# The second one-hot table of the gate spread: one comparison on VectorE, its four parts multiplied by the gates on ScalarE

## The reference

```python
fv, fpos = lax.top_k(cand.reshape(T, PEER_HEADS, PEER_TOPK * PEER_TOPK), PEER_TOPK)
gates = jax.nn.softmax(fv, axis=-1).astype(h.dtype)
u = jnp.take(U, ic, axis=0)
act = jax.nn.gelu(jnp.einsum('chkd,cd->chk', u, xc), approximate=False)
vv = jnp.take(V, ic, axis=0)
return jnp.einsum('chk,chkd->cd', gc * act, vv)
```

## Time and profile before

| | |
|---|---|
| median of 3 runs | 2122.65 us (2121.01 to 2124.01) |
| the profiled execution: time, span | 2123.55 us, 2121.8 us |
| mean granted TensorE clock | 0.961 |
| busy over the span | PE 90%, PEld 75%, DVE 67%, ACT 35%, POOL 27% |

### The profile page before, as it was taken

One profiled execution on the slowest core, in us unless ns is written; L12 is line 12 of the kernel. 1 busy time (PEld: TensorE's weight loads), 2 busy tenths in 40 slices (PEclk: granted clock), 3 DMA queues, 4 the chain that ended last, 5 costly groups with the idle time before them and its releaser, 6 DMA issues.

```text
span 2121.8 us, 33140 instructions
## 1 busy us (share of the span) xinstructions
PE 1911.8 (90%) x10322; PEld 1599.3 (75%) x10322; DVE 1424.2 (67%) x2902; ACT 733.0 (35%) x1304; POOL 569.5 (27%) x435
## 2 busy tenths in 40 slices
PE   2889896786877999999999999996999999999995
PEld 2343585675733787879999999996998888888884
DVE  4187535435334577775688888884768888888886
ACT  1221224333312343435444444341243333333331
POOL 3011422031101232314422322323424333333311
PEclk9999998998988999999999999998999999999998
DMA  7373100000050333334699988889979999999981
GB/s 265 103 247 100 40 1 1 0 0 0 0 210 30 116 112 110 120 100 155 226 305 301 304 300 300 288 277 342 342 273 413 354 357 357 349 350 361 354 284 53
DMA packets 244203, 434.82 MB, mean 205 GB/s; under 512 B 84578, under 2 KB 157636, under 8 KB 244164
## 3 DMA queue, kind: packets, MB, share of 16 engines
q1 hardware_dynamic: 207300, 300.12, 40.9%
q0 software_dynamic: 36864, 134.23, 17.6%
HBM read 379.77 MB, written 54.53 MB: 205 GB/s over the span
## 4 chain that ended last, share of the span: by engine, by line
PE 64%; DMA 1%; DVE 1%; issue 1%; ACT 0%; POOL 0%; SPq 0%; POOLq 0%; ACTq 0%; DVEq 0%
PE bank L1318 25%; PE bank L1709 8%; PE bank L1710 8%; PE bank L1711 8%; PE bank L1298 5%; PE bank L1646 5%; PE bank L1692 4%; DMA urows<-in_peer_u 1%; PE bank L1658 1%; DMA gates<-SS 0%; POOL wide L1626 0%; DVE n_stats L1118 0%; DVE wide L2012 0%; DVE wide L2010 0%; DVE wide L1128 0%
## 5 line engine op out<-in xcount | busy, mean ns | idle before, releaser
L1318 PE MATMUL bank<-hh,uh 128*128 128x384 f32 x1024 | 358.3, 350 | 0.0
L1318 PE MATMUL bank<-hl,uh 128*128 128x384 f32 x1024 | 344.6, 337 | 0.0
L1709 PE MATMUL bank<-vh,wh 128*128 128x512 f32 x768 | 299.1, 389 | 3.1 <-DVE wl L1971 3.1
L1711 PE MATMUL bank<-vh,wl 128*128 128x512 f32 x768 | 299.0, 389 | 0.0
L1710 PE MATMUL bank<-vl,wh 128*128 128x512 f32 x768 | 299.0, 389 | 0.0
L1376 POOL DMA_INDIRECT vsel<-in_peer_v,picks x128 | 153.6, 1200 | 425.5 <-DVE gt L1402 411.5
L1805 ACT ACTIVATE vh<-vraw 128x1024 fp32r<-128x1024 f32 x128 | 135.9, 1061 | 287.7 <-PE bank L1711 272.6
L1376 POOL DMA_INDIRECT usel<-in_peer_u,picks x108 | 146.7, 1359 | 247.5 <-DVE usel L1383 233.9
L1968 DVE TENSOR_TENSOR vl<-vraw,vh 128x1024 fp32r<-128x1024 f32 x128 | 156.7, 1224 | 81.7 <-ACT vh L1805 81.7
L1318 PE MATMUL bank<-hh,ul 128*128 128x384 f32 x1024 | 198.4, 335 | 0.0
L1318 PEld LDWEIGHTS bank<-hl,uh 128*128 128x128 f32 x1024 | 194.4, 190 | 0.0
(11 more groups left out here) (314 smaller groups left out, 3106.2 us busy)
## 6 DMA issues: line engine op xcount, KB each, us to landing
urows<-in_peer_u SPq DMA_DIRECT2D x128, 512.0 KB, 7.8
vraw<-in_peer_v SPq DMA_DIRECT2D x128, 512.0 KB, 6.1
ada<-in_ada_w SPq DMA_DIRECT2D x12, 2048.0 KB, 8.7
scored<-act_out SPq DMA_DIRECT2D x128, 192.0 KB, 4.2
gates<-SS SPq DMA_DIRECT2D x16, 1536.0 KB, 13.0
gtile<-gates SPq DMA_DIRECT2D x32, 768.0 KB, 7.3
act_in<-scored SPq DMA_DIRECT2D x128, 192.0 KB, 6.2
wt<-in_w_in SPq DMA_DIRECT2D x19, 512.0 KB, 3.9
```

Source lines behind the costliest of these rows:

```text
L1318: last = pe.matmul(bank, u[:, k, :], h[:, k, :], start=(n == 0), stop=(n == 3 * KD - 1))
L1709: pe.matmul(b, wh[s][:, cols], vh[s][:, half], start=first, stop=False)
L1711: last = pe.matmul(b, wl[s][:, cols], vh[s][:, half], start=False, stop=stop)
```

## The change

VectorE makes all four parts of OJ with one comparison of 128x512, as it did for OI, and raises a new semaphore `ones_up`. ScalarE, once it has copied row s+1, waits for it, multiplies the four parts of each step of row s in place by their gates, and raises `hot`, on which TensorE waits as before.

```diff
@@ ScalarE, for each row s, behind the copies of row s+1 and the small Gelu
+                        for q in steps_of(s):
+                            n = STEPS * (i - SPREAD) + q
+                            act.wait_ge(ones_up, START + n + 1)
+                            for k in range(4):
+                                last = act.activation(OJ[q % SLOTS][:, k, :], OJ[q % SLOTS][:, k, :], ACT.Copy,
+                                                      scale=turned[2][:, bass.ds(4 * n + k, 1)])
+                            last.then_inc(hot, 1)
                         for q in steps_of(s):
                             act.wait_ge(spread, START + 2 * STEPS * b + (STEPS * o + q + 1))
@@ VectorE, hot_step
-                for k in range(4):
-                    at = bass.ds(4 * n + k, 1)
-                    last = dve.tensor_scalar(OJ[q % SLOTS][:, k, :], iota[:, :], turned[1][:, at], turned[2][:, at],
-                                             ALU.is_equal, ALU.mult)
-                last.then_inc(hot, 1)
+                dve.tensor_tensor(OJ[q % SLOTS], iota[:, :].unsqueeze(1).broadcast_to([P, 4, P]),
+                                  turned[1][:, bass.ds(4 * n, 4)].unsqueeze(2)
+                                  .broadcast_to([P, 4, P]), ALU.is_equal).then_inc(ones_up, 1)
```

More of the change, by code:

```diff
@@ L1485, in emit_experts @@
             sem(n) for n in ("less_up", "exp_up4", "gate_up4", "t_up4", "t_out4"))
-        hot, spread, staged = sem("hot"), sem("spread"), sem("staged")
+        ones_up, hot, spread, staged = sem("ones_up"), sem("hot"), sem("spread"), sem("staged")
         sent = [sem(f"sent{b}") for b in range(2)]
```

## The result

The changed kernel took 2153.33 us (median of 4 runs, 2148.18 to 2155.02), the kernel before 2123.09 us beside it: a ratio of 1.014, 95% interval 1.0121 to 1.0159. That is 30 us slower. I had said 2152.

What follows compares the result with a forecast made beforehand. TensorE was taken to bound the gate spread, VectorE's relief being worth 0; new TensorE waits of 14.0 + 4.6 + 10.6 = 29.2 us on 2123.55 gave 2152 us, 1.4% slower, with 8 in 10 from 2135 to 2172.

Steps and rivals of the forecast that it cites:

- What bounds the stage: Gate spread: TensorE busy for 390.00 of 390 us, so VectorE's relief of some 41 us is worth 0.
- The price of the multiplications: ScalarE in the spread: 384 activations of 0.39 us alone, 0.29 a step; four end after 1.26 us.
- Where they stand: Multiplications of row s queue behind copies of row s+1, which await TensorE's transposes; they race 12 or 24 matmuls.
- the three waits of 0.58, 0.66 and 2.00 us: TensorE's waits for the table: row 0 of odd blocks, row 2 of any block, row 0 of even blocks.
- the sum: TensorE's added waits in the spread: 14.0 + 4.6 + 10.6 = 29.2 us; with its bounds, chance 0.75.
- not caught up: A late table delays everything queued on TensorE, and so the next copies; each wait therefore adds in full.
- Row 1 behind the second table load: Row 1 of an even block: tables up at 1238.38 against TensorE's load at 1238.46, a wait of 0.
- The first block: TensorE at half clock takes 5.28 us, 2.64 more than at full; that covers the 2.00, so 7 even blocks count.
- The table load: ScalarE's 1.28 us load ahead of even blocks' copies, without the skill's drain of about 1380 ns.
- It passes through: Behind the spread, TensorE's 20.58 us wait for rows of U moves with the last block and swallows nothing.
- The clock: Rival: TensorE's clock falls to half behind the waits, 18.5 us more at 7 places, 2170 us; chance 0.11.
- The rival "faster": VectorE's 41 us brings gathers sooner and shrinks the wait for U; 2117 us if multiplications are hidden; chance 0.04.

Runs made afterwards that it cites:

- dve_both: Changed kernel with ScalarE's multiplications taken out and done by VectorE as one 128x512 multiplication after its comparison; 2123.25 us, 1.0005 of the kernel before.
- ahead_early_unrolled: Changed kernel, first-step multiplications ahead of next row's copies, VectorE making next block's first table before row 3's adds, ScalarE's loop written out; 2124.19 us, 0.9994 of before.
- ahead: Changed kernel with the multiplications of each row's first step placed ahead of the next row's copies on ScalarE; 2149.10 us, 1.0115 of the kernel before.
- ahead_unrolled: Changed kernel with first-step multiplications ahead of the next row's copies and ScalarE's spread loop written out; 2133.31 us, 1.0037 of the kernel before.
- twice: Changed kernel with four more ScalarE activations per step ahead of the real ones, into an unread buffer; 2211.61 us, 1.0420 of the kernel before.
- unrolled: Changed kernel with ScalarE's loop over the gate spread written out, removing two table loads per second block; 2143.41 us, 1.0090 of the kernel before.

## Why the prediction was right

- **What bounds the stage**: right. TensorE has no gap in `dve_both`, with VectorE busier, nor in the kernel before. The load on VectorE moved the stage by 0.1 us; with VectorE relieved and the waits gone (`ahead_early_unrolled`) it was 0.4 us longer, not shorter.
- **The price of the multiplications**: 0.39 us alone and 0.29 a step by the estimate, 0.41 and 0.29 measured. The slope was taken a little low, as 0.88 ns for 128 columns is 113 and not 108 ns, which changes nothing at this size. One sign was wrong: ScalarE's busy time was to rise by 140 to 150 us and rose by 111.2. Activations that overlap count once, so it is the step of 0.29 and not the length of 0.39 that adds up; the prediction had the 111 us itself, further up.
- **Where they stand**: the three waits of 0.58, 0.66 and 2.00 us measured 0.63, 0.65 and 2.06, in 8, 16 and 7 places as counted. The positions were read rightly, but not what sets them: the prediction has the copies of row s+1 wait for TensorE's transposes. In the kernel before they hardly ever do (0.5 us of idle time over 126 copies). ScalarE waits for the last table product of the row before, copies it and does a Gelu, and the copies follow at once. That wait is for TensorE too, so the sum and "not caught up" hold all the same. Row 1 behind the second table load, forecast with 0.08 us to spare, did not wait. The sum was 29.2, the loads' waits 29.8 and the stage's growth 29.0.
- **The first block**: rightly without a wait, but half clock is not all of the reason. In the changed kernel its table load ran from 1019.89 to 1021.17 beside the transposes, and the copies began at 1021.34; the first four multiplications were done at about 1024.0, and TensorE loaded at 1025.48. Elsewhere TensorE gets from the transposes to line 1692 in 2.89 us (1226.67 to 1229.56 in the kernel before). By these rows I estimate a wait of 0.4 us at full clock, not 2.00. Full clock would also save 5.28 - 2.89 = 2.39 us there and not the 2.64 of the prediction, which halved all of it.
- **The table load**: 1.28 us with nothing behind it. The changed kernel's copies start at 1242.92, 0.01 us after the load's end at 1242.91, so the drain that the Trainium skill adds for a switch to another set ("ScalarE: Activation LUTs", What ACT_TABLE_LOAD costs) shows nowhere on this path. Without the table loads the stage lost 10.5 us; 7 x (2.06 - 0.63) is 10.0.
- **It passes through**: the wait for rows of U behind the spread was 19.82 us, against 20.58. The chain that ended last, in order of time, of the changed kernel (start us, us):

```profile
1460.77 8.36 DMA gates<-SS
1475.49 19.82 DMA urows<-in_peer_u
1497.40 5.76 PE bank L1318 x24
```

- **The clock**: rightly a rival, and rightly not the likeliest. It was nearer than the time tells: with 1.16 us more in each wait it is there.
- **The rival "faster"** fell: VectorE's 41 us, and the 29 by which the stage is longer, went into its own waits, which in the window of the stage are 390 - 277.24 = 113 us now against 53 before.
- **Not seen by the prediction**: how VectorE stands towards ScalarE. I called its comparison early because ScalarE was not free, which is true of the changed kernel only. `ahead` showed that it is late once ScalarE is ready sooner. The prediction of the change did not rest on it, my expectations of `ahead` and `ahead_unrolled` did.

The 1.4 us of the span outside the stage lie mostly in TensorE's clock behind the wait for U: the first 24 matmuls there take 5.76 us (last line above) where those of the kernel before take 4.79, 0.97 us less. The granted clock was 0.50 until about 1469.6 before, 3.2 us after the rows came, and until about 1500.6 in the changed kernel, 5.2 us after. The rest is 0.1 us ahead of the stage and 0.4 behind these matmuls. Whether it differs from run to run stays open.

## What to carry to other kernels

Price work that is moved from a relieved engine to an idle one by its place, not by the engine's busy share: ScalarE was busy 41% of the stage, and 1.3 us put between two things that TensorE asks of it in turn cost TensorE 29 us over 31 waits. Look for what the new instruction stands behind (here the copy of a result that TensorE has just made, a Gelu, the copies of the next row, and a table load that had been free), and for the next engine in the row before moving it forward. Where the bounding engine has no gap, do not expect more than no change: here even that took two further moves and a written-out loop.

## What the runs showed of the hardware

- Gaps of 2.90 us between matmuls, in work whose other gaps were 0.8 and 1.5 us (`twice`), brought the granted clock to its half level (1.2 of 2.4 GHz) six times of seven; behind the other one it stayed at 1.00. Gaps of 1.74 us beside others of 0.33 (the changed kernel) never did.
- A matmul behind a wait starts with its weight load (1245.28 and 1245.29 in the changed kernel) where in dense work the load leads by 0.17 us. The same wait shows as 2.06 us on the load and as 1.74 on the matmul.
- The instruction that works out an address ahead of each activation costs nothing here: 8 activations take 2.44 us with it and in `unrolled`, without it, too, and the waits there are the same 0.6 us.
- A table load of 1.28 us is followed by the next activation within 0.02 us, and it costs nothing where nothing late stands behind it: with the loop written out 15 of the 16 in the stage are gone from the kernel before, and its time is 0.9999 (0.9989 to 1.0008) of what it was.
